# A two-layer hybrid decoder step: the loop over the layers written out on three engines

## The reference

```python
for l in range(DEPTH):
    xn = _rmsnorm(hp, norm_mix[l])
    q_s, k_s, v_s, q_r, k_r, v_r, g_r = _project(xn, w_in[l], pos_p)
    ...
    o_swa = _swa_attend(q_s, k_band, v_band, qpos_p, kpos_p, sinks[l], rel_bias)
    o_ret, st_p = _retention_prompt(q_r, k_r, v_r)
    hp = _mix_out(hp, o_swa, o_ret, g_r, w_o[l])          # x + W_o [swa || gated retention]
    hp = _ffn(hp, norm_ffn[l], w_gate_up[l], w_down[l])   # x + W_down (silu(a) * b)
    ...   # the same for the 8 x 4 sampled tokens, with cache and state
y_prompt = _rmsnorm(hp, norm_final)
```

## Time and profile before

| | before |
|---|---|
| runs, median (lowest to highest) | 2682.03 us (2680.91 to 2684.4) |
| profiled execution | 2685.05 us |
| its span | 2683.5 us, 53800 instructions |
| mean granted clock of PE | 0.995 |
| PE busy | 2630.4 us, 98% |
| DVE, ACT, POOL busy | 1491.9, 1249.6, 174.5 us |
| moved by DMA | 459.02 MB, mean 171 GB/s |

### The profile page before, as it was taken

How to read it: one execution, slowest core, us unless ns; L and a number is a source line. 1 busy time by engine, 2 the same in 40 slices (tenths; PEclk the granted TensorE clock), 3 DMA queues, 4 the chain that set the end, 5 groups by cost and what they waited for, 6 DMA issues and landing times.

```text
span 2683.5 us, 53800 instructions
## 1 busy us (share of the span) xinstructions
PE 2630.4 (98%) x19722; PEld 2596.1 (97%) x19722; DVE 1491.9 (56%) x2387; ACT 1249.6 (47%) x2237; POOL 174.5 (7%) x222
## 2 busy tenths in 40 slices
PE   6999999999999999999999999999999999999997
PEld 6999999999999999999999999999999999999997
DVE  6566665555555555444455666555555555545445
ACT  4455554444444444444444555444444444444443
POOL 5300001000000000000020000110000000000000
PEclk9999999999999999999999999999999999999998
DMA  6655555555555555555555555554555555555554
GB/s 209 202 196 188 186 175 174 160 165 164 162 169 164 157 171 164 160 164 162 163 184 168 192 195 194 186 161 153 171 164 164 164 164 164 164 159 163 164 168 141
DMA packets 429939, 459.02 MB, mean 171 GB/s; under 512 B 19349, under 2 KB 418029, under 8 KB 429872
## 3 DMA queue, kind: packets, MB, share of 16 engines
q1 hardware_dynamic: 407488, 404.38, 49.2%
q0 software_dynamic: 18400, 48.42, 5.3%
q10 hardware_dynamic: 3984, 5.34, 0.6%
HBM read 436.12 MB, written 27.54 MB: 173 GB/s over the span
## 4 chain that ended last, share of the span: by engine, by line
PE 60%; issue 33%; DVE 3%; DVEq 1%; DMA 1%; POOLq 1%; ACT 1%; ACTq 0%; POOL 0%; SPq 0%
PE ps L982 19%; PE ps L984 18%; PE ps L986 18%; DVE w_lo L650 1%; DVE xg_lo L662 1%; DMA new_rs<-st 1%; PE ps L1223 1%; PE ps L1160 1%; PE ps L1232 1%; DVEq L910 1%; DMA raw<-w_in 0%; PE ps L1181 0%; ACT w_hi L363 0%; PE ps L1147 0%; POOLq L1309 0%
## 5 line engine op out<-in xcount | busy, mean ns | idle before, releaser
L650 DVE TENSOR_TENSOR w_lo<-raw,w_hi 128x512 fp32r<-128x512 f32 x1572 | 1067.3, 687 | 910.9 <-ACT w_hi L363 892.6
L363 ACT ACTIVATE w_hi<-raw 128x512 fp32r<-128x512 f32 x1572 | 960.9, 620 | 1105.3 <-PE ps L986 1085.8
L982 PE MATMUL ps<-xg_hi,w_hi 128*128 128x288 f32 x4224 | 1259.2, 298 | 18.7 <-DVE w_lo L650 14.5
L984 PE MATMUL ps<-xg_lo,w_hi 128*128 128x288 f32 x4224 | 1249.2, 296 | 0.0
L986 PE MATMUL ps<-xg_hi,w_lo 128*128 128x288 f32 x4224 | 1248.3, 296 | 0.0
L982 PEld LDWEIGHTS ps<-xg_hi,w_hi 128*128 128x128 f32 x4224 | 795.2, 188 | 25.7 <-DVE w_lo L650 12.6
L984 PEld LDWEIGHTS ps<-xg_lo,w_hi 128*128 128x128 f32 x4224 | 796.5, 189 | 0.5
L986 PEld LDWEIGHTS ps<-xg_hi,w_lo 128*128 128x128 f32 x4224 | 795.6, 188 | 0.0
L982 PE MATMUL ps<-cat_hi,w_hi 128*128 128x288 f32 x1024 | 305.5, 298 | 9.2 <-DVE w_lo L650 8.8
L984 PE MATMUL ps<-cat_lo,w_hi 128*128 128x288 f32 x1024 | 303.2, 296 | 0.0
L986 PE MATMUL ps<-cat_hi,w_lo 128*128 128x288 f32 x1024 | 303.0, 296 | 0.0
(11 more groups left out here) (201 smaller groups left out, 1241.8 us busy)
## 6 DMA issues: line engine op xcount, KB each, us to landing
raw<-w_gate_up SPq DMA_DIRECT2D x352, 512.0 KB, 3.6
raw<-w_in SPq DMA_DIRECT2D x178, 512.0 KB, 3.6
raw<-w_down SPq DMA_DIRECT2D x160, 512.0 KB, 3.7
raw<-w_o SPq DMA_DIRECT2D x64, 512.0 KB, 3.9
st<-state POOLq DMA_DIRECT2D x16, 1024.0 KB, 7.9
new_rs<-st POOLq DMA_DIRECT2D x16, 1024.0 KB, 5.9
raw<-w_down SPq DMA_DIRECT2D x32, 256.0 KB, 2.9
yT<-x_res ACTq DMA_DIRECT2D x4, 576.0 KB, 3.1
```

The lines of the kernel that those rows point to most:

```text
L363: nc.scalar.activation(w_hi[q][:, 0:n, :], raw[s][:, n * (j % 2):n * (j % 2) + n, :], ACT.Copy).then_inc(hi_ready[q], 1)
L650: nc.vector.tensor_tensor(w_lo[q][:, 0:n, :], raw[s][:, n * (j % 2):n * (j % 2) + n, :], w_hi[q][:, 0:n, :].bitcast(F32), ALU.subtract).th ...
L982: nc.tensor.matmul(out, w_hi[q][:, t, cols], x_hi[:, x, :], start=(k == 0), stop=False, skip_group_check=True)
L984: nc.tensor.matmul(out, w_hi[q][:, t, cols], x_lo[:, x, :], start=False, stop=False, skip_group_check=True)
```

## The change

In the programs of ACT, DVE and PE the loop over the layers becomes a loop of Python, so that its body stands twice in the instruction stream, with the layer as a constant in each copy. The shorter loops inside stay loops on the chip, now two of each. SP and POOL keep their loops over the layers.

```diff
--- before.py
+++ after.py
@@ -417,7 +417,7 @@
             nc.scalar.activation(sink_s[:], ps[0:64, 5, 0:DEPTH], ACT.Copy).then_inc(bank_read[5], 1)
             act.drain().then_inc(rows_ready, 1)
 
-            with act.Fori(0, DEPTH) as layer:
+            for layer in range(DEPTH):
                 r0 = layer * ROUNDS
 
                 split_on(r0, LEAD + 1, 6)
@@ -688,7 +688,7 @@
                                     x_res[:, 3 * KT // 4:, :], ALU.mult).then_inc(sq_ready, KT // 2)
             dve.wait_ge(consts_loaded, 16)
 
-            with dve.Fori(0, DEPTH) as layer:
+            for layer in range(DEPTH):
                 r0 = layer * ROUNDS
                 split_on(r0, LEAD + 1, 6)
                 reciprocal_std("rms_mix", layer)
@@ -1011,7 +1011,7 @@
             nc.tensor.matmul(ps[0:64, 5, 0:DEPTH], table("head_rows", HEADS), setup_rows[:, XLEN:XLEN + DEPTH],
                              start=True, stop=True).then_inc(setup_filled, 1)
 
-            with pe.Fori(0, DEPTH) as layer:
+            for layer in range(DEPTH):
                 r0 = layer * ROUNDS
 
                 def in_pair(r, a, n, j0=0, j1=8, first=False):
```

## The result

The changed kernel takes 2668.21 us (median of 4 runs, 2666.82 to 2669.4) against 2683.22 for the kernel before (median of 4, 2680.91 to 2684.85): 15.0 us less, a ratio of 0.994 with a 95% interval of 0.9927 to 0.9953. Forecast were 2674.5 us and a range of 2670.5 to 2680.

A forecast was written before the change was run, and what follows sets the result against it. The kernel was taken as matmul-bound, PE busy 98% of the span. Gains of 6.55 (boundary), 0.72 (projection) and 0.2 (norm) made 7.5 us, so 2682.03 - 7.5 = 2674.5 us, range 2670.5 to 2680.

The forecast's parts named there:

- The layer boundary: Between layers 1 and 2, PE's 3.91 us stop and the next round's 2.64 us slowdown both vanish: gain 6.55 us.
- The cover: In layer 2's first round, DVE writes the fifth eighth of the split weights 0.71 us before PE wants it.
- first rival: PE falls through, but ACT or DVE stop for new code and weight eighths come late: 2677.1 us, chance 0.11.
- The output projection: Even-pair rounds fall from 13.33 to odd pairs' 13.21 us, three rounds in each of two layers: gain 0.72 us.
- The attention loop: PE is busy 70.98 of each 71.04 us turn, so nothing to gain: 0, bound 0.5 us.
- The start: ACT's first table load at program start goes, but 6.8 us of cover hides it: gain 0, bound 0.47 us.
- The third projection round: PE waits on splits behind squares awaiting POOL's sums; untouched, but the clock may shift: 0, plus or minus 2.9 us.
- Rivals 2, 3 and 4: 2: PE stops at new code, 0.05; 3: an inner loop refetches every turn, slower, 0.04; 4: no effect, 0.02.
- norm: Feed-forward's first turn, the round with the norm, loses register instructions: 0.1 us a layer, 0.2 in all (0 to 0.4).

The follow-up runs named there:

- the one without ACT: PE's and DVE's layer loops written out against the kernel before, ACT keeping its loop; 2669.77 us, ratio 0.9941.
- the kernel with two idle increments: Changed kernel with two idle semaphore increments on DVE between the two low parts of x of each output projection pair; 2674.12 us.

## Why the forecast had the right sign and half the size

**The layer boundary: right.** 6.6 us measured, 6.55 forecast. No wait of PE is left in the trace between 1330 and 1355 us, the first round of layer 2 takes 12.74 us at a clock of 1.00, and the table loads of line 363 are gone. The cover came out as worked out too: DVE writes the fifth eighth from 1340.94 on, 5.01 us after the round began, as in the down loop's turn:

```profile
1340.94 1.88 DVE L650 TENSOR_TENSOR w_lo<-raw,w_hi 128x512 fp32r<-128x512 f32 x3
```

In the traces of the kernel with PE alone and of the one without ACT, which keep ACT's jump and table load, PE waits 1.9 and 2.5 us there, at a mean clock of 0.90 over the round. So the first rival's mechanism exists; with the jumps of all three engines gone it does not occur. A kernel in which DVE alone keeps its jump was not run.

**The output projection: the step that failed.** "In the changed order even pairs have what odd pairs have now. So the gain is 13.33 - 13.21 = 0.12 us, for three rounds in each of two layers: 0.72." It was 5.8. I had taken the odd rounds' 13.21 for the floor, though a fed round takes 12.80, and had counted register instructions instead of asking what each start runs into. The rows had the hint: PE busy 13.07 of 13.21, so odd rounds lost time too. What stood behind it was GpSimd's addition, which I never set beside the low parts. With 0.07 to 0.08 us less of register work in each of two places, the second low part passes in front of the addition in even and odd rounds alike, and 0.41 to 0.53 us a round goes, in all six. Six rounds with the whole loss gone, in place of three with the difference between two kinds of rounds: that is the forecast's missing 5.1 us.

**The attention loop: 0 forecast (bound 0.5), 1.1 measured.** One turn fell from 71.04 to 70.86 us. It goes with DVE: the kernel with DVE alone written out has it (70.9), the one with PE alone has not. PE's busy time, 70.98 of 71.04, hides such waits, since a product of some 0.3 us overlaps the next ones. The gap between starts would have shown it: in the second turn it fell from 0.44 to 0.27 us ahead of the product behind the first scores (at 187.91 before, 185.73 after), which is the gain of a turn.

**The start: 0 forecast, 1.9 in this trace**, but not by the change: of the twelve traces two have the short first round, this one and that of DVE alone, where the first product was late as well (16.20 and 16.30 us); seven others with DVE written out, the changed kernel's second one among them, have 22.7 or 22.8.

**The third projection round: 0 plus or minus 2.9 forecast, 0.3 measured**, layer by layer -1.9 and +1.6, as wide as said. The cause that it gave, GpSimd's late sums, is what ends last in the trace; the late weights ahead of them were not looked at.

**Rivals 2, 3 and 4** are out: PE falls through without a stop, no inner loop's branch took over 0.24 us, and the end moved. Rival 1 was priced with a stall that left the clock at 1.00; with PE alone written out a wait of 1.9 us came with a mean clock of 0.90, and the round cost 16.44 - 12.80 = 3.6 us more. The forecast also took the window of two blocks as PE's. The section that it names there, in the Trainium skill, "Runtime: NRT & Kernel Launch", "Instruction fetch mechanics", gives PE 2048 instructions, enough for a loop of some 1,000, so the short branches of the earlier trace rows do not speak against it.

What is left: boundary, projection, attention and norm make 13.6 us. The medians differ by 15.0 and, measured a second time, by 16.7 (2684.32 to 2667.57). Start and third round move from run to run by as much as the rest (over the ten traces that keep the copies where they were, a third round takes 15.3 to 19.5 us); that this explains it is not shown.

## What to carry to other kernels

Where a round is slower than the fed round, name the operation that is slow before pricing a change to the round; here a duration of 0.52 or 1.09 us of one and the same instruction said it. When two engines get in each other's way, a change of 0.03 to 0.1 us in who starts first can be worth more than the instructions that it saves, so a forecast of shorter issue times has to look at what each start now passes or meets. Judge a nearly busy engine by the gaps between starts, not by its busy share.

## What the runs showed of the hardware

- The order between DVE and GpSimd is settled within hundredths of a microsecond: 0.05 us ahead in the records, the low part takes 0.51 and the addition 1.13; 0.02 ahead (the kernel with two idle increments), 1.14 and 0.81. So a recorded start does not tell the winner that closely.
- ACT took 1.30 and 9.51 us to issue two strided copies of 992 KB between tensors in device memory, and computed nothing for 10.6 us. GpSimd had issued the same two in 4.2 us, and then stood in its next drain (20.8 us in layer 1 of the changed kernel).
- Written-out code cost no wait at the layer boundary: PE, ACT and DVE ran from one copy of the body into the other with 0.13 us between PE's products.
